# A split running sum for blockwise stick-breaking attention: two triangle products, masks as matmuls, clip and high part on GpSimd

## The reference

```python
z = einsum('bqhd,bkhd->bhqk', q, k) * scale + bias
log_beta = log_sigmoid(z)
log_1m = where(mask, log_sigmoid(-z), 0.0)
tail = cumsum(log_1m, axis=ax, reverse=True) - log_1m
a = where(mask, exp(log_beta + tail), 0.0)
out = einsum('bhqk,bkhd->bqhd', a, v)
```

## Time and profile before

| | |
|---|---|
| median of 3 runs | 3238.76 us |
| lowest, highest | 3236.3, 3241.75 us |
| the profiled execution's own time | 3242.27 us |
| its span | 3240.5 us |
| PE busy in the span (modelled ends) | 2925.6 us, 90% |
| VectorE busy | 1532.7 us, 47% |
| ScalarE busy | 760.0 us, 23% |
| GpSimd busy | 1061.7 us, 33% |
| mean granted clock of TensorE | 0.948 of 2.4 GHz |
| attention, first z to last output | about 1678 to 2147 us of the span |

### The profile page before, as it was taken

The page is one execution under the profiler, slowest core; times in us unless marked ns, Lnnn a source line. Parts: engine busy times, 40 slices in busy tenths (PEclk is TensorE's granted clock), DMA queues, the critical chain, the costliest instruction groups (busy, mean ns, idle before and its releaser), DMA issues.

```text
span 3240.5 us, 45834 instructions
## 1 busy us (share of the span) xinstructions
PE 2925.6 (90%) x16032; PEld 2638.1 (81%) x16032; DVE 1532.7 (47%) x2610; ACT 760.0 (23%) x1575; POOL 1061.7 (33%) x932
## 2 busy tenths in 40 slices
PE   5999679999999999899888888888999999999997
PEld 3777458999999999899875555566989999999997
DVE  5699964333322223641438888830152322222336
ACT  4111062200000000231227777730031000000002
POOL 2478913232222223222224444411223222223220
PEclk9999889999999999999989999975799999999999
DMA  3000001111111111144252222222211111111111
GB/s 115 27 26 20 15 26 53 40 52 40 46 40 47 40 40 52 40 140 129 73 143 66 64 65 68 59 84 91 79 40 53 46 40 40 46 40 40 47 46 54
DMA packets 87687, 184.02 MB, mean 57 GB/s; under 512 B 28995, under 2 KB 43715, under 8 KB 87268
## 3 DMA queue, kind: packets, MB, share of 16 engines
q1 hardware_dynamic: 64260, 145.00, 13.6%
q10 hardware_dynamic: 23264, 36.61, 3.7%
HBM read 150.59 MB, written 30.99 MB: 56 GB/s over the span
## 4 chain that ended last, share of the span: by engine, by line
PE 71%; DVE 13%; issue 9%; ACT 4%; POOL 1%; ACTq 1%; DVEq 1%; DMA 0%; POOLq 0%; SPq 0%
PE bank L1229 47%; PE bank L1335 14%; DVE cv L980 3%; DVE s_sb L1137 2%; PE bank L1483 2%; PE bank L1455 2%; PE bank L1274 2%; DVE sh_sb L1149 1%; DVE xg L925 1%; PE bank L1437 1%; DVE xl L929 1%; DVE ssq L915 1%; ACT sh_sb L844 1%; DVE rstd L1128 1%; POOL s_sb L541 1%
## 5 line engine op out<-in xcount | busy, mean ns | idle before, releaser
L1229 PE MATMUL bank<-xh,wh 128*128 128x352 f32 x3456 | 1134.6, 328 | 54.5 <-DVE xl L929 22.4
L1229 PE MATMUL bank<-xh,wl 128*128 128x352 f32 x3456 | 1118.8, 324 | 0.0
L1229 PE MATMUL bank<-xl,wh 128*128 128x352 f32 x3456 | 1118.5, 324 | 0.0
L498 POOL CAST wh<-w_raw 128x1024 fp32r<-128x1024 f32 x188 | 302.5, 1609 | 1717.1 <-PE bank L1229 1401.3
L1229 PEld LDWEIGHTS bank<-xh,wh 128*128 128x128 f32 x3456 | 656.2, 190 | 70.6 <-issue 41.1
L1229 PEld LDWEIGHTS bank<-xl,wh 128*128 128x128 f32 x3456 | 659.1, 191 | 1.8 <-issue 1.7
L1229 PEld LDWEIGHTS bank<-xh,wl 128*128 128x128 f32 x3456 | 657.3, 190 | 0.0
L500 POOL TENSOR_TENSOR wl<-w_raw,wh 128x1024 fp32r<-128x1024 f32 x188 | 455.2, 2421 | 15.1
L1047 DVE TENSOR_TENSOR hf<-bank,sg 128x352 f32<-128x352 f32 x132 | 69.2, 524 | 770.5 <-ACT sg L731 770.5
L1335 PE MATMUL bank<-hh,wh 128*128 128x352 f32 x1056 | 350.0, 331 | 57.5 <-DVE x L1058 55.0
L731 ACT ACTIVATE sg<-bank 128x352 f32<-128x352 f32 x132 | 61.3, 464 | 1277.9 <-PE bank L1229 1277.8
(11 more groups left out here) (136 smaller groups left out, 3138.0 us busy)
## 6 DMA issues: line engine op xcount, KB each, us to landing
w_raw<-wstream SPq DMA_DIRECT2D x188, 512.0 KB, 3.2
k_sb<-k_split SPq DMA_DIRECT2D x16, 512.0 KB, 3.5
qh_sb<-q_split SPq DMA_DIRECT2D x64, 128.0 KB, 2.6
ql_sb<-q_split SPq DMA_DIRECT2D x64, 128.0 KB, 2.7
kp<-cache_kt SPq DMA_DIRECT2D x16, 512.0 KB, 3.3
vp<-cache_v SPq DMA_DIRECT2D x16, 512.0 KB, 3.4
x<-x_t ACTq DMA_DIRECT2D x3, 1408.0 KB, 11.9
k_t<-stage ACTq DMA_DIRECT2D x8, 528.0 KB, 2.8
```

What stands on the lines that cost most here:

```text
L498: pool.tensor_copy(wh[:, s], w_raw[:, s % RAW]).then_inc(w_hi, 1)
L1229: mm = pe.matmul(out, a[:, slot, w], b[:, k, tgs(tg)], start=(k == 0 and i == 0), stop=(k == KC - 1 and i == 2))
```

## The change

`carry` and the mask instructions go. The high part and the low part that the triangle product multiplies are now those of a running sum: `att_sum` on VectorE adds to the new maximum, in place and from column carry0 on, the previous step's running sum (`sums`, three buffers). The triangle times the new running sum gives, for each key, the sum over partitions at or after it, of this block and of all later blocks together; what is missing is the later blocks' share of the partitions before it, and a second, strict triangle (`neg_stri_r`) times the previous step's high and low parts adds that. So the f32 product with `carry` becomes two fp32r products. The masks become one fp32r product of 128 columns per diagonal step, identity times a matrix of -1e30 on the masked triangle, added to z, so that both exps give zero there. GpSimd takes over the high part for all steps (`att_s_hi`) and the clip. The leads of z, exp, clip, ln, the maximum and both parts are one smaller; those of cum, the weights and the value product stay. Three constants are made by GpSimd and copied to fp32r by VectorE.

The diff's core (left out: the definitions of semaphores and buffers, the counting in `attention_steps`, and initial increments):

```diff
-LEAD = 6
+LEAD = 5
+MASKED = -1e30
...
+def sums_until(t):
+    return STEPS[t]["sums"] + 2 - (0 if t >= 0 else NSUM)
...
-    carry = halves(ssq) + halves(xg[:].rearrange("p a t -> p (a t)"))
+    sums = halves(ssq) + halves(xg[:].rearrange("p a t -> p (a t)"))[:1]
...
+        pool.wait_ge(n_kv.ready, NTG * KC)
+        pool.memset(strict_src, -1.0).then_inc(Att.const_src, 1)
+        pool.memset(mask_src, MASKED).then_inc(Att.const_src, 1)
+        pool.wait_ge(Att.const_src, 2)
+        pool.affine_select(out=strict_src, in_=strict_src, compare_op=ALU.is_ge, fill=0.0, base=-1,
+                           pattern=[[1, P]], channel_multiplier=-1).then_inc(Att.const_src, 1)
+        pool.affine_select(out=mask_src, in_=mask_src, compare_op=ALU.is_ge, fill=0.0, base=0,
+                           pattern=[[-1, P]], channel_multiplier=1).then_inc(Att.const_src, 1)
+        def att_s_hi(it, t):
             s, g = STEPS[t], it * NSTEP + t
-            if s["diag"]:
-                wait_alone(pool, Att.s, g + 3)
-                strict_mask(s_sb[:, t % 3, s["c0"]:s["c0"] + P]).then_inc(Att.s_mask, 1)
-        def att_carry(it, t):
+            c0 = s["c0"]
+            if s["first"]:
+                pool.wait_ge(Att.s, g + 3)
+            else:
+                pool.wait_ge(Att.sum, it * NSUM + sums_until(t))
+            wait_alone(pool, Att.cum, g + 2)
+            pool.tensor_copy(sh_sb[:, t % 3, c0:QT], sums[t % 3][:, c0:QT]).then_inc(Att.sh, 1)
+        def att_clip(it, t):
             s, g = STEPS[t], it * NSTEP + t
-            if s["first"] or s["last"]:
-                return
-            cols = slice(s["carry0"], QT)
-            pool.wait_ge(Att.cum, g + 1)
-            pool.wait_ge(Att.s, g + 3)
-            pool.wait_ge(Att.block, it * NBLOCK + STEPS[t - 1]["blocks"])
-            pool.wait_ge(Att.carry, it * NCARRY + (STEPS[t - 1]["carries"] + 2))
-            pool.tensor_tensor(carry[(t + 1) % 4][:, cols], carry[t % 4][:, cols], s_sb[:, t % 3, cols], ALU.add)\
-                .then_inc(Att.carry, 1)
-        def att_a_mask(it, t):
-            s, g = STEPS[t], it * NSTEP + t
-            if s["diag"]:
-                wait_alone(pool, Att.a, g + 1 + NZ)
-                strict_mask(a_sb[:, t % 3, s["c0"]:s["c0"] + P]).then_inc(Att.a_mask, 1)
+            tile = soft[t % 2][:, s["c0"]:QT]
+            wait_alone(pool, Att.exp, g + 1)
+            pool.tensor_scalar(tile, tile, EXP_CLIP, None, ALU.min).then_inc(Att.clip, 1)
         for n in range(2):
             pool.wait_ge(v_stored[n], 16 * (3 * KC // 6))
         pool.memset(v_sb[:, :, DH:2 * DH], 0.0).then_inc(Att.v_zero, 1)
-        attention_slots(pool, ((att_a_mask, 1), (att_carry, 4), (att_s_mask, 5)))
+        attention_slots(pool, ((att_s_hi, 3), (att_clip, 5)))
...
-        attention_slots(act, ((att_weights, 1), (att_s_hi, 4), (att_ln, 5), (att_exp, 6), (att_out, 0)))
+        attention_slots(act, ((att_weights, 1), (att_ln, 4), (att_exp, 5), (att_out, 0)))
...
-            v.wait_ge(Att.carry, it * NCARRY + (carries_before(t, 3) + 2))
-            v.scalar_tensor_tensor(out=s_sb[:, t % 3, c0:QT], in0=Z[t % NZ][:, c0:QT], scalar=b_sb[:, e:e + 1],
+            v.wait_ge(Att.sum, it * NSUM + sums_until(t - 2))
+            v.scalar_tensor_tensor(out=sums[t % 3][:, c0:QT], in0=Z[t % NZ][:, c0:QT], scalar=b_sb[:, e:e + 1],
                                    in1=soft[t % 2][:, c0:QT], op0=ALU.add, op1=ALU.max).then_inc(Att.s, 1)
         def att_s_lo(it, t):
             s, g = STEPS[t], it * NSTEP + t
             c0 = s["c0"]
-            if t % 2:
-                if s["diag"]:
-                    v.wait_ge(Att.s_mask, it * NMASK + s["masks"])
-                else:
-                    v.wait_ge(Att.s, g + 3)
-                v.wait_ge(Att.cum, g + 1)
-                v.tensor_copy(sh_sb[:, t % 3, c0:QT], s_sb[:, t % 3, c0:QT]).then_inc(Att.sh[1], 1)
-            v.wait_ge(Att.sh[t % 2], it * HSTEP + (t // 2 + 1))
-            v.tensor_tensor(sl_sb[:, t % 3, c0:QT], s_sb[:, t % 3, c0:QT], sh_sb[:, t % 3, c0:QT].bitcast(F32),
+            v.wait_ge(Att.sh, g + 1)
+            v.wait_ge(Att.cum, g + 2)
+            v.tensor_tensor(sl_sb[:, t % 3, c0:QT], sums[t % 3][:, c0:QT], sh_sb[:, t % 3, c0:QT].bitcast(F32),
                             ALU.subtract).then_inc(Att.sl, 1)
-        def att_block(it, t):
+        def att_sum(it, t):
             s, g = STEPS[t], it * NSTEP + t
-            if s["diag"] and not s["last"]:
-                block = slice(s["c0"], s["c0"] + P)
-                v.wait_ge(Att.s_mask, it * NMASK + s["masks"])
-                v.wait_ge(Att.cum, g + 1)
-                v.tensor_copy(carry[(t + 1) % 4][:, block], s_sb[:, t % 3, block]).then_inc(Att.block, 1)
+            if s["first"]:
+                return
+            cols = slice(s["carry0"], QT)
+            v.wait_ge(Att.s, g + 3)
+            if not STEPS[t - 1]["first"]:
+                v.wait_ge(Att.sum, it * NSUM + sums_until(t - 1))
+            v.tensor_tensor(sums[t % 3][:, cols], sums[(t - 1) % 3][:, cols], sums[t % 3][:, cols], ALU.add)\
+             .then_inc(Att.sum, 1)
         def att_out(it, t):
             s = STEPS[t]
         for n in range(2):
             v.wait_ge(q_stored[n], 4 * 16 * (KC // 2))
-        attention_slots(v, ((att_s_lo, 4), (att_block, 4), (att_max, 5), (att_clip, 6), (att_out, 0)))
+        v.wait_ge(Att.const_src, 4)
+        v.tensor_copy(neg_stri_r[:], strict_src).then_inc(Att.const, 1)
+        v.tensor_copy(mask_r[:], mask_src).then_inc(Att.const, 1)
+        v.tensor_copy(ident_r[:], ident[:]).then_inc(Att.const, 1)
+        attention_slots(v, ((att_s_lo, 3), (att_max, 4), (att_sum, 4), (att_out, 0)))
...
-            pe.matmul(Z[t % NZ][:, c0:QT], k_sb[:, e, keys], ql_sb[:, cols], start=False, stop=True)\
-              .then_inc(Att.z, 1)
+            mm = pe.matmul(Z[t % NZ][:, c0:QT], k_sb[:, e, keys], ql_sb[:, cols], start=False, stop=True)
+            if s["diag"]:
+                mm = pe.matmul(Z[t % NZ][:, c0:c0 + P], ident_r[:], mask_r[:], start=False, stop=True,
+                               skip_group_check=True)
+            mm.then_inc(Att.z, 1)
         def att_cum(it, t):
             s, g = STEPS[t], it * NSTEP + t
                 mm = pe.matmul(Z[t % NZ][:, c0:QT], neg_tri_r[:], part[:, t % 3, c0:QT], start=False, stop=True,
                                skip_group_check=True)
             if not s["first"]:
-                pe.wait_ge(Att.block, it * NBLOCK + STEPS[t - 1]["blocks"])
-                if not STEPS[t - 1]["first"]:
-                    pe.wait_ge(Att.carry, it * NCARRY + (STEPS[t - 1]["carries"] + 2))
-                mm = pe.matmul(Z[t % NZ][:, cr:QT], neg_one[:], carry[t % 4][:, cr:QT], start=False, stop=True,
-                               skip_group_check=True)
+                for part in (sh_sb, sl_sb):
+                    mm = pe.matmul(Z[t % NZ][:, cr:QT], neg_stri_r[:], part[:, (t - 1) % 3, cr:QT], start=False,
+                                   stop=True, skip_group_check=True)
             mm.then_inc(Att.cum, 1)
         def att_av(it, t):
                 pe.wait_ge(Att.v_in[e], it * 32 + 32)
             if s["first"]:
                 pe.wait_ge(Att.o_lo, it * 4 + (2 * e + s["qt"] + 1))
-            if s["diag"]:
-                pe.wait_ge(Att.a_mask, it * NMASK + s["masks"])
-            else:
-                pe.wait_ge(Att.a, g + 1 + NZ)
+            pe.wait_ge(Att.a, g + 1 + NZ)
             pe.matmul(DN[s["qt"]][:, c0:QT], v_sb[:, s["b"], DH * e:DH * e + P], a_sb[:, t % 3, c0:QT],
                       start=s["first"], stop=s["last"], skip_group_check=True).then_inc(Att.av, 1)
         pe.wait_ge(consts, 8)
         pe.wait_ge(l_q.out, l_q.base + 6 + NTG * KC)
         pe.wait_ge(Att.v_zero, 1)
-        attention_slots(pe, ((att_z, 6), (att_cum, 2), (att_av, 0)))
+        pe.wait_ge(Att.const, 3)
+        attention_slots(pe, ((att_z, 5), (att_cum, 2), (att_av, 0)))
```

More of the change, by code:

```diff
@@ L97, in attention_steps @@
                                   carry0=min(QT, c0 + P) if b >= qt * (QT // P) else 0))
-    masks = carries = blocks = 0
+    sums = 0
     for s in steps:
-        masks += s["diag"]
-        carries += not (s["first"] or s["last"])
-        blocks += s["diag"] and not s["last"]
-        s["masks"], s["carries"], s["blocks"] = masks, carries, blocks
+        sums += not s["first"]
+        s["sums"] = sums
     return steps
```

46 lines of the change are left out of this document (12 added, 34 removed).

## The result

The changed kernel takes 3305.52 us (median of 4 runs, 3304.3 to 3312.5) against 3237.53 for the kernel before: ratio 1.0218, 95% interval 1.0192 to 1.0245, 68 us slower. The forecast was slower, at 3263, with a range to 3305, which the result passes by half a microsecond. The profiled execution took 3305.37 us, its span is 3303.6. Up to 1640 us the windows of the two kernels agree, so attention is read as before.

What follows compares the result with a forecast made beforehand. Before the change, ScalarE and VectorE handing each step back and forth was taken to delay PE. Afterwards VectorE's loop with GpSimd: 16 x (29.6 - 28.2) = +22 us, start +2, sum +24, giving 3263 us; range 3220 to 3305.

Steps and rivals of the forecast that it cites:

- part 4: Attention's cast, low part, maximum, sum run one after the other: 27.2 us a half, 1.0 below the kernel before.
- part 5: GpSimd's clip behind the cast blocks VectorE's low part: 3.15 us over 12 steps, 2.4 taken, 29.6 a half.
- Part 3: GpSimd in attention does one cast and one clip per step, each priced 0.56 us at 512 columns.
- the dearer case: Rival: GpSimd's operations or wakes in attention cost more, up to +86 us with a two-input-priced clip; chance 0.15.
- both deductions: Low-part blocking in a half: two first steps escape (2 x 0.26 us), two second ones are on the edge (2 x 0.38).
- Part 1: PE's work in attention falls from 22.7 to 21.1 us a half, without gain as PE won't be the bound.
- the third rival: PE's clock falls in attention: +224 us at the lower level, +10 or so for a tenth of the time; chance 0.04.
- Part 6: At attention's start PE waits for three constant copies on VectorE: about +2 us, ends 0 and 4.
- The rival "VectorE wins the port (faster)": At each cast's end the low part goes first, clip hidden under the maximum: 27.2 us a half, 3225 us; chance 0.20.

Runs made afterwards that it cites:

- a4: The changed kernel without any clip, exp taking half of z: 3253.6 us, ratio 1.0062 to the kernel before.
- a2: The changed kernel with a same-size copy on GpSimd in the clip's place, exp taking half of z: 3273.09 us, ratio 1.0106.
- a14: The changed kernel with exp of step k+5 ahead of ln of step k+4 on ScalarE: 3276.27 us, ratio 1.0135.
- a8: The changed kernel without the 128-column mask products on PE, masks left out: 3307.5 us, ratio 1.0208.
- a12: The changed kernel with clip on VectorE, low part last, four buffers per part, constants copied after the first stored-queries wait: 3257.29 us, ratio 1.0063.
- a6: The changed kernel with the clip on VectorE and the low part last there: 3249.27 us, ratio 1.0032.
- a5: The changed kernel with VectorE's order changed to maximum, sum, low part: 3299.95 us, ratio 1.0181.

## Why the prediction was right and wrong

The sign was right, for reasons that hold only in part; the size was off, 68 us for 24. Of +4.06 us a half, the runs give +1.00 to the loop (a4), where part 4 had -1.0, and +3.06 to the clip, where part 5 had +2.4. So of the 2.7 us a half by which the forecast was short, 2.0 are the loop, and only 0.7 the clip; but the clip's term is near by luck. With a copy at the assumed price it is 1.51 (a2 less a4), 0.9 below part 5, and the clip's own form adds 1.55 (after less a2).

- **Part 3, GpSimd's prices: the first step that failed.** The cast was nearly right (0.61 for 0.56). The clip was priced like the cast, "as both have one input, like the nearest row"; it takes 1.50 in the mean. The upper end, the two-input add's 1.28, was nearer but also too low. With a copy at 0.61 in the clip's place the kernel takes 3273 us (a2), 10 from the forecast; the clip itself brings the other 32. The prediction called this the less sure price and put the dearer case at 0.15 and up to +86 us. The Trainium skill (GPSIMD Engine Reference, section 4.1) calls one-input operations roughly line-rate. The copy's 0.61 us for 512 columns agrees, the clip's 1.50 does not.
- **Part 4, the loop: the second step that failed, in its size.** The order cast, low part, maximum, sum is there, and the chain of waits in attention goes through just these four. It comes to 29.2 us a half instead of 27.2. Casts are 0.05 to 0.09 us dearer (0.29, 0.40, 0.50, 0.61): 2 x (0.09 + 0.08 + 0.06) + 6 x 0.05 = 0.8. The sum starts 0.12 us behind the maximum's end (1817.12 + 0.75 to 1817.99), not 0.04: ten times 0.08, 0.8. About 0.4 of the 2.0 is left without a name.
- **Part 5, the collision.** The mechanism is real: for a copy as forecast (a2: 1.07 us; step 3.39; half 30.72), for the clip with two differences. It holds VectorE for its first 0.47 us at 512 columns, not for its whole length, and behind a cast it starts 0.08 us after the cast's end, too late against the low part (a14). In the changed kernel at full width it doesn't even come to the contest, because each clip delays ln, exp and so the next one. What is held there are sums, in the narrow steps. The 2.4 us of part 5 and the missing 0.9 us of price at full width stood in each other's place, and the forecast came nearer than its reasons deserved: that is luck. The 2.4 itself was a choice, between the 3.15 of the sum and the 1.87 that remain when both deductions are taken in full.
- **What the prediction left out** is the ring clip, ln, exp, clip over ScalarE and GpSimd. Part 4 followed one loop and showed that engines' sums "fit beneath". Here two loops of different stations alternate, each last at other widths, and a half costs more than the one alone (a4's loop 29.21; the whole 32.27). That the ring is a large part of the difference a14 shows; how large exactly it doesn't, as the holds change with it. With a clip of 0.56 the same turn would take 2.91 - 1.49 + 0.56 = 1.98 us, an estimate, and at full width stay beneath.
- **Part 1 and PE.** Right: PE has gaps, the scores' wait is gone, and taking PE work away changes nothing (a8). The clock did fall, from 1.00 to 0.96 in the window, as the third rival said, by which a tenth of the time at the lower level costs 10 us; it cost about 4.
- **Part 6, the start.** z begins at 1694.18, 0.6 us behind the last constant's copy begun at 1693.55. But VectorE's wait for the stored queries also ended later in this execution, at 1693.27 against 1689.18 before, and a12 doesn't resolve the 2 us. 68 - 65 leaves 3 us for it and for the spread of the runs.
- **The rival "VectorE wins the port (faster)"** had its condition come true at full width (the low part takes 0.69, the clip is late), and it didn't make the kernel faster: its 27.2 us a half rested on part 4's sum and on a cheap clip.

## What to carry to other kernels

Before an operation is moved to GpSimd, its price there has to be seen for that very form: copy, min with a constant and two-input add differ by a factor of 2.4, and for how long each of them stops VectorE is a second question beside the duration. Look for every loop that goes through the moved instruction, queue by queue, and compare them width by width: two loops that are each affordable as a sum over the steps can alternate as the bound. And an order found good for one placement (exp ahead of ln) must be tried again after the next move.

## What was unexpected of the hardware

- On GpSimd a minimum of f32 with a constant takes 1.49 us at 128x512, undisturbed 1.17 at 384, 0.84 at 256 and 0.52 at 128 columns; a copy or a cast to fp32r takes 0.61 at 512, an add of two tiles 1.28. VectorE does the same clip in 0.42 (a6). The Trainium skill (GPSIMD Engine Reference, section 3.1) has 769 ns for a loop over 512 elements: the copy is below it, the clip about twice it.
- GpSimd's copy and add hold up VectorE's instructions with two SBUF inputs until 0.14 or 0.15 us before their own end (1.07 and 1.76 us for 0.69). Its minimum with a constant holds them for a first part alone: at 512 columns until 0.47 us after its start, at 384 until 0.36, at 256 until 0.25; a copy held them as long, 0.47 at 512 and 0.25 at 256. A VectorE instruction that starts later is left alone. The largest delays seen are a sum of 256 columns at 0.88 for 0.42 and a low part of 512 at 1.10 for 0.69 (a5). The minimum is itself drawn out, to 1.99 us, when it starts under a low part.
- Which of two released instructions comes first is decided by hundredths: behind a cast a copy starts 0.05 us before the cast's nominal end, an add 0.04 before, the minimum 0.08 after; VectorE's low part starts 0.03 after.
- The length of PE's wait alone does not tell whether the granted clock falls. Two waits of the changed kernel, at the same place of the pattern:

```profile
1836.51 0.50 PE L1398 MATMUL bank<-sh_sb,neg_tri_r 128*128 128x512 f32 x1 [1.74 <-DVE sl_sb L1124]
...
1900.45 0.79 PE L1398 MATMUL bank<-sh_sb,neg_tri_r 128*128 128x512 f32 x1 [1.74 <-DVE sl_sb L1124]
```

  Behind the first the clock is 1.00, behind the second 0.50 for some 3 us. In a4, where PE's waits for the low part were up to 1.8 us for weights and 1.5 for products, it stood at 1.00 in all of 1750 to 2150 us.
